# Compressed-branch scores of a two-layer decoder trunk: from eight fp32r matmuls against zero-padded keys to four native fp32 matmuls of 32 columns

## The chip, the cores and the metric

One core of one Trainium2 chip runs the kernel. The time is the device time of one execution in microseconds; lower is better. The kernel before took 349.9 us (median of 3 runs, 349.83 to 349.91).

## What is computed

A decoder trunk of two layers over 256 tokens of width 1024, all in float32. Layer 0 is native sparse attention (16 heads of 64, in 4 groups of 4 heads that share keys and values), layer 1 is a gated linear recurrence (HGRN2). The change lies in the compressed branch of layer 0: blocks of 32 keys, 16 apart, are compressed to 15 keys for each group, rotated, and scored against the queries:

```python
k_cmp = rope(compress(kc, pe_k, wk1, wk2), cmp_end)            # 15 keys per group of heads
sc = einsum('bqgrd,bngd->bqgrn', q, k_cmp) * scale             # r: 4 heads of group g
p_c = masked_softmax(sc, cmp_end[None, :] <= t[:, None])
o_c = einsum('bqgrn,bngd->bqgrd', p_c, v_cmp)
o = g0 * o_c + g1 * o_s + g2 * o_w                             # with selected and window branches
```

With 4 blocks of 64 to select and 16 to be selected, the selected branch takes all blocks, so the scores serve the softmax of the compressed branch only.

## The kernel before

The program is one list of steps (`schedule()`, written out by hand), and every engine walks through this list in the same order and does its own part of each step, with semaphores between them. TensorE's part decides the pace. Big projections are done in "fp32r", a format of 4 bytes that TensorE takes in one pass at reduced precision: each operand is split into a high part (a ScalarE copy, `w_hi`, L889) and a low part (a VectorE subtraction, `w_lo`, L1103), and three matmuls hi·hi, hi·lo, lo·hi are added in PSUM (steps `pa` with 512 moving columns, `pb` with 256). A weight unit is 1024x512, loaded by SyncE into one of two raw buffers and split in four quarters. When a quarter's two parts are ready, `lo_done` counts up, and TensorE's matmuls of that quarter wait for it. `SPREAD` says after which step of the list each quarter is split.

The queries are rotated by VectorE, GpSimd and ScalarE (`rp`, `stg`) and turned by TensorE in the steps `stage`; ScalarE copies them to `q2[128, head, token]`, whose partitions 0 to 63 hold the high parts of the 64 dimensions of a head and 64 to 127 the low parts. So one contraction over 128 partitions against a key that stands there twice gives (q_hi + q_lo)·k.

The compressed keys go through these steps: `cmp2` of the keys (VectorE rotates them, then writes the doubled high part and the doubled low part to `kcs`, L1260 and L1262), `kcT` (two transposes on TensorE, L745; eight ScalarE copies of 32 columns to `kc_pad`, L977), and `sc`, once for each tile i of 128 queries (L618, called at the `sc` branch). `kc_pad[128, part, group, 128]` holds, for each group, its 32 key columns at their own place and zeros elsewhere. The zeros are set by a GpSimd memset at the start (L1431). Eight matmuls (4 groups x 2 parts) of 512 moving columns (4 heads x 128 queries) add up in one bank: each writes all 128 output rows, and contributes to the 32 rows of its group.

```python
for g in range(G):
    for part in range(2):
        m = mm(ps[:], kc_pad[:, part, g], q2[:, g * R:(g + 1) * R, i * P:(i + 1) * P],
               g == 0 and part == 0, g == G - 1 and part == 1)
```

The order of the list around it: `cmp2` of the values, `stage` 6 (its queries are the last that tile 0 needs), three slices of the z projection (weight units U_Z0 and U_Z1, 16 slices of 12 matmuls in all, taken one after the other as `filler`), `sc` 0, two slices, `stage` 7, `scT` 0 (transposes of the scores), two slices, `sc` 1, three slices, `scT` 1, three slices, `pcT` 0 (transposes of the probabilities), the first item `s` 0 of the other branches, two slices, `pcT` 1, the items `s` 1 to 3, the last slice, and then the 24 items of the selected and window branches. Steps `sc`, `scT` and `pcT` 0 share bank 7. After `sc` ScalarE copies the scores out (L983), after `scT` VectorE adds the mask and does the softmax (L1280 to L1295) with the exponentials on ScalarE (L990). In VectorE's own order the split of the last quarter of U_Z1 stands right behind the softmax of tile 0.

Other native fp32 matmuls in the kernel: `cmp1` (output in halves of 64 rows, `w` and `zT`), the products with the values (`pv`, `prob_t` and `v_tok`, halves of 64 rows too, and `vc_bd` over all 128), and layer 1's `qa`, `kb`, `attn`. In the trace each native fp32 matmul shows as two weight loads and two matmuls, here called its two passes; a fp32r matmul shows as one.

Of the kernel before, what the change touches and what calls it, by code (L numbers as in the profile page):

```python
# [21 lines left out]
P = 128  # L22
# [5 lines left out]
H, G, R, HD = 16, 4, 4, 64  # L28
CB, CS, NC, NP_ = 32, 16, 15, 32
# [8 lines left out]
F32 = mybir.dt.float32  # L38
FR = mybir.dt.float32r
BF16 = mybir.dt.bfloat16  # L40
U8 = mybir.dt.uint8
ALU = mybir.AluOpType
ACT = mybir.ActivationFunctionType
# [257 lines left out]
def program(nc, t_in, out):  # L301
    with ExitStack() as ctx:
        def sb(name, shape, dt=F32, scope=ctx):
            return scope.enter_context(nc.sbuf_tensor(name, shape, dt))
# [10 lines left out]
        ident = sb("ident", [P, P])  # L315
        ident_r = sb("ident_r", [P, P], FR)
# [21 lines left out]
        nsa = ExitStack()  # L338
# [4 lines left out]
        q2 = sb("q2", [P, H, S], FR, nsa)  # L343
        k2 = sb("k2", [P, 2, 2, G, S], FR, nsa)
        v_tok = sb("v_tok", [P, TT, 2, G, HD], F32, nsa)
        kc_pad = sb("kc_pad", [P, 2, G, P], FR, nsa)
        vc_bd = sb("vc_bd", [P, 2, P], F32, nsa)
        zT = sb("zT", [P, KT, S], F32, nsa)

# [5 lines left out]
        pre = ExitStack()  # L355
# [3 lines left out]
        hidT = sb("hidT", [P, 2, 2, P], F32, pre)  # L359
        kcr = sb("kcr", [P, 3, HD], F32, pre)  # L360
        tri = kcr[:, 0:2].rearrange("p a d -> p (a d)")
        kcs = sb("kcs", [P, 2, P], FR, pre)
        wg = sb("wg", [P, KT, 48], F32, pre)
        wg_hi = sb("wg_hi", [P, KT, 48], FR, pre)
        wg_lo = sb("wg_lo", [P, KT, 48], FR, pre)
# [77 lines left out]
        kc_v = sem("kc_v")  # L443
        zeros = sem("zeros")
# [40 lines left out]
        def taken(key):  # L485
            return drained[USES[key][0]]
# [25 lines left out]
        def bc(ap, n, at):  # L512

            shape = list(ap.shape)
            return ap.unsqueeze(at).broadcast_to(shape[:at] + [n] + shape[at:])
# [100 lines left out]
        def _(pe):  # L616
            def mm(o, lhsT, rhs, start, stop):
                return nc.tensor.matmul(o, lhsT, rhs, start=start, stop=stop, skip_group_check=True)  # L618
# [16 lines left out]
            for n, (step, banks) in enumerate(SCHEDULE):  # L635
                kind = step[0]
                key = bank_key(step)
# [7 lines left out]
                ps = bank[b]  # L645
# [5 lines left out]
                if kind == "hT":  # L651
# [8 lines left out]
                    for j in range(per_bank):  # L660
                        c = (per_bank * q + j) * P
                        m = nc.tensor.transpose(ps[:, j * P:(j + 1) * P], src[:, c:c + P], ident[:])
                elif kind == "gc":
                    pe.wait_ge(ident_in, 16)
                    pe.wait_ge(g_cols_in, 16)
                    m = nc.tensor.transpose(ps[:, 0:KT], g_rows[0:KT], ident[0:KT, 0:KT])
                elif kind == "rs":
                    pe.wait_ge(ones_set, 1)
                    pe.wait_ge(diag_set, TT)
                    for t in range(TT):  # L670
                        m = mm(ps[:, t * P:(t + 1) * P], ones, diag[:, t], t == 0, t == 1)
                elif kind == "pa" and step[1] == 0:

                    _, u, t, sl = step
# [6 lines left out]
                    for j, kk in enumerate(two):  # L681
# [3 lines left out]
                        m = mm(ps[:], h_lo[:, kk, t * P:(t + 1) * P], w_hi[:, u, kk], False, kk == KT - 1)  # L685
                elif kind == "pa":

                    _, u, t, sl = step
                    if sl == 0:
                        act_ready(0 if u <= U_O1 else 1, t, u)  # L690
                    for kk in (2 * sl, 2 * sl + 1):
# [4 lines left out]
                        m = mm(ps[:], h_lo[:, kk, t * P:(t + 1) * P], w_hi[:, u % 2, kk], False, kk == KT - 1)  # L696
                elif kind == "pb":

                    _, u, m2, sl = step
# [4 lines left out]
                    for kk in range(4 * (sl % 2), 4 * (sl % 2) + 4):  # L704
# [5 lines left out]
                        m = mm(o, cols(w_lo), h_hi[:, kk], False, kk == KT - 1)  # L710
                elif kind == "stage":
# [5 lines left out]
                    for c in range(4):  # L717
                        m = nc.tensor.transpose(ps[:, c * P:(c + 1) * P].bitcast(FR), stg[:, j % 2, 4 * half + c], ident_r[:])  # L718
                elif kind == "cmp1":
# [5 lines left out]
                    for j in range(CS):  # L725
                        half = slice((j % 2) * HD, (j % 2 + 1) * HD)
                        m = mm(ps[half, 0:CH], flat[:, kv, j].rearrange("p g n -> p (g n)"), w1[:, j], j < 2, j >= CS - 2)
                elif kind == "cmpT":
# [4 lines left out]
                    for c in range(2):  # L733
                        m = mm(ps[:, c * HD:(c + 1) * HD], hid[:, c * P:(c + 1) * P], fold[:], c == 0, c == 1)
                elif kind == "cmp2":
# [4 lines left out]
                    for c in range(2):  # L740
                        m = mm(ps[:, 0:HD], hidT[:, kv, c], w2[:, kv, c], c == 0, c == 1)
                elif kind == "kcT":
                    pe.wait_ge(kc_v, 1)
                    for c in range(2):
                        m = nc.tensor.transpose(ps[:, c * P:(c + 1) * P].bitcast(FR), kcs[:, c], ident_r[:])  # L745
                elif kind == "gl":
                    pe.wait_ge(wg_lo_d, 1)
                    for kk in range(KT):
                        mm(ps[0:48, 0:S], wg_hi[:, kk], h_hi[:, kk], kk == 0, False)
                        mm(ps[0:48, 0:S], wg_hi[:, kk], h_lo[:, kk], False, False)  # L750
                        m = mm(ps[0:48, 0:S], wg_lo[:, kk], h_hi[:, kk], False, kk == KT - 1)
                elif kind == "glT":
                    wait_taken(pe, ("gl",))
                    for t in range(TT):
                        m = nc.tensor.transpose(ps[:, t * 48:(t + 1) * 48], gT[:, t * P:(t + 1) * P], ident[0:48, 0:48])
                elif kind == "sc":
                    i = step[1]
# [3 lines left out]
                        for half in range(2):  # L761
                            wait_taken(pe, ("stage", j, half))
                    for g in range(G):
                        for part in range(2):
                            m = mm(ps[:], kc_pad[:, part, g], q2[:, g * R:(g + 1) * R, i * P:(i + 1) * P],
                                   g == 0 and part == 0, g == G - 1 and part == 1)
                elif kind == "scT":
                    i = step[1]
                    wait_taken(pe, ("sc", i))
                    for r in range(R):  # L770
                        m = nc.tensor.transpose(ps[:, r * P:(r + 1) * P], s_ct[:, r * P:(r + 1) * P], ident[:])
                elif kind == "pcT":
                    i = step[1]
                    pe.wait_ge(cmp_scaled, i + 1)
                    for r in range(R):
                        m = nc.tensor.transpose(ps[:, r * P:(r + 1) * P], s_c[:, i, r * P:(r + 1) * P], ident[:])
                elif kind == "s":
                    i, gp, g, rp_, br = ITEMS[step[1]]
# [11 lines left out]
                    if i == 0:  # L790
                        m = mm(ps[:], ident_b[:], bc(tri_b[:], 4, 1), False, True)
                    else:
                        m = mm(ps[:].rearrange("p (r k q) -> p r k q", r=2, k=2)[:, :, 1], ident_b[:], bc(tri_b[:], 2, 1), False, True)
# [84 lines left out]
        def _(act):  # L878
# [26 lines left out]
            for n, (step, _) in enumerate(SCHEDULE):  # L905
                kind, key = step[0], bank_key(step)
                if LAST.get(key) == n:
                    ps = bk(key)
# [50 lines left out]

                            load_w1(act, "v")  # L960
                    elif kind == "cmpT":
                        act.wait_ge(zeros, 3)
                        wait_full(act, key)
                        nc.scalar.activation(hidT[:, step[1]].rearrange("p c (g n) -> p (c g) n", g=G)[:, :, 0:CS],
                                             ps[:, 0:2 * HD].rearrange("p (c n) -> p c n", n=CS), ACT.Silu).then_inc(taken(key), 1)
# [4 lines left out]
                        wait_full(act, key)  # L970
                        nc.scalar.activation(gate[:], ps[:, 0:TT * 48].rearrange("p (t c) -> p t c", t=TT), ACT.Copy).then_inc(taken(key), 1)
                    elif kind == "kcT":
                        act.wait_ge(zeros, 3)
                        wait_full(act, key)
                        for part in range(2):
                            for g in range(G):
                                m = nc.scalar.activation(kc_pad[:, part, g, g * NP_:(g + 1) * NP_],  # L977
                                                         ps[:, part * P + g * NP_:part * P + (g + 1) * NP_], ACT.Copy)
                                if part == 1 and g == G - 1:
                                    m.then_inc(taken(key), 1)  # L980
                    elif kind == "sc":
                        wait_full(act, key)
                        nc.scalar.activation(s_ct, ps[:], ACT.Copy).then_inc(taken(key), 1)  # L983
# [100 lines left out]
        def _(dve):  # L1084
            steps = [0]

            def step_(ins):

                ins.then_inc(vec_step, 1)
                steps[0] += 1  # L1090

            def settled():

                dve.wait_ge(vec_step, steps[0])
# [69 lines left out]
            for n, (step, _) in enumerate(SCHEDULE):  # L1164
                kind, key = step[0], bank_key(step)
                if LAST.get(key) == n:
# [81 lines left out]
                    elif kind == "cmp2" and step[1] == 0:  # L1248
# [6 lines left out]
                        wait_taken(dve, key)  # L1255
                        step_(V.tensor_tensor(kcr[:, 2], kcr[:, 0], kcr[:, 1], ALU.add))
                        settled()
                        hi2 = kcs[:, 0].rearrange("p (u d) -> p u d", u=2)
                        lo2 = kcs[:, 1].rearrange("p (u d) -> p u d", u=2)
                        step_(V.tensor_copy(hi2, bc(kcr[:, 2], 2, 1)))  # L1260
                        settled()
                        V.tensor_tensor(lo2, bc(kcr[:, 2], 2, 1), hi2.bitcast(F32), ALU.subtract).then_inc(kc_v, 1)  # L1262
                    elif kind == "cmp2":
                        dve.wait_ge(zeros, 3)
                        wait_full(dve, key)
                        for g in range(G):
                            m = V.tensor_copy(vc_bd[g * NP_:(g + 1) * NP_, g // 2, (g % 2) * HD:(g % 2 + 1) * HD],
# [159 lines left out]
        def _(pool):  # L1427
            GP = nc.gpsimd
            row = lambda ap: ap.unsqueeze(0).broadcast_to([P, D])
            GP.memset(hidT[:], 0.0).then_inc(zeros, 1)  # L1430
            GP.memset(kc_pad[:].bitcast(F32), 0.0).then_inc(zeros, 1)  # L1431
            GP.memset(vc_bd[:], 0.0).then_inc(zeros, 1)


# [125 lines left out]
```

## Time and profile before

| | before |
|---|---|
| median of 3 runs | 349.9 us (349.83 to 349.91) |
| profiled execution: its own time | 349.11 us |
| its span | 346.5 us |
| TensorE busy | 331.5 us (96%) |
| VectorE busy | 235.4 us (68%) |
| ScalarE busy | 178.4 us (51%) |
| GpSimd busy | 93.2 us (27%) |
| mean granted clock of TensorE | 0.996 of full |

The profiled execution has 2.6 us around its span (349.11 less 346.5), and its own time lies 0.8 us below the median. Starts are counted from the start of the span. A matmul's length in the trace holds its pipeline and overlaps the next ones, so what a matmul costs is read from one start to the next. PE is TensorE, PEld its weight loads, DVE VectorE, ACT ScalarE, POOL GpSimd.

### The profile page before, as it was taken

The page shows a single profiled execution, that of the slowest core. Times are in us where ns is not written, and L with a number is a line of the kernel's source. Part 1 is how long each engine was busy: PE and PEld are TensorE (multiplying, and loading weights), DVE is VectorE, ACT ScalarE, POOL GpSimd, SP SyncE. Part 2 cuts the span into 40 slices and gives each one's busy share as a digit, 9 for nine tenths or more (in the row PEclk, how much of TensorE's full clock was granted, in tenths as well). Part 3 has the DMA queues.
Part 4 walks back from the last instruction along what each step waited for, and adds up shares of the span by engine and source line. Part 5 has one row for each costly group of instructions (what it writes and reads, how often), then busy time and mean ns, then how long its engine had stood idle before and what let it go on. Part 6 is the DMA issues. An engine that isn't in the chain of part 4 may idle for free.

```text
span 346.5 us, 5690 instructions
## 1 busy us (share of the span) xinstructions
PE 331.5 (96%) x2157; PEld 280.7 (81%) x2157; DVE 235.4 (68%) x400; ACT 178.4 (51%) x369; POOL 93.2 (27%) x83
## 2 busy tenths in 40 slices
PE   8999999899799978999999999999999999999993
PEld 5789788678799945676678788999999999889882
DVE  2978957608677498977536835547386996899942
ACT  4966069245561787886517616647353100067621
POOL 2003021523200246574400010050080675533000
PEclk9999999999999999999999999999999999999998
DMA  7999999920747500060530673944636033001011
GB/s 281 380 320 194 329 278 214 316 96 0 163 81 143 103 0 2 13 231 1 193 112 0 215 265 120 311 176 145 214 129 243 1 114 130 2 0 60 3 61 61
DMA packets 28474, 49.37 MB, mean 142 GB/s; under 512 B 3160, under 2 KB 7648, under 8 KB 28448
## 3 DMA queue, kind: packets, MB, share of 16 engines
q1 hardware_dynamic: 25696, 44.82, 41.6%
q10 hardware_dynamic: 2240, 2.17, 3.6%
q0 software_dynamic: 512, 2.03, 1.6%
q8 instruction: 17, 0.28, 0.3%
q14 instruction: 9, 0.07, 0.1%
HBM read 47.97 MB, written 1.05 MB: 141 GB/s over the span
## 4 chain that ended last, share of the span: by engine, by line
PE 73%; DVE 9%; ACT 7%; issue 5%; DMA 2%; POOL 2%; SPq 0%; DVEq 0%; ACTq 0%
PE bank L618 68%; DVE w_lo L1103 4%; PE bank L798 3%; DMA raw<-in_nsa 2%; POOL rp L1450 2%; ACT prob L1009 2%; ACT w_hi L889 2%; ACT h_hi L896 1%; PE bank L718 1%; DVE prob_t L1312 1%; DVE nmax L1300 1%; DVE rp L1211 1%; ACT q L951 1%; ACT w_hi L915 1%; PE bank L859 1%
## 5 line engine op out<-in xcount | busy, mean ns | idle before, releaser
L1103 DVE TENSOR_TENSOR w_lo<-raw,w_hi 128x1024 fp32r<-128x1024 f32 (+1 forms) x80 | 92.8, 1201 | 25.3 <-ACT w_hi L889 25.2
L618 PE MATMUL bank<-w_hi,h_hi 128*128 128x512 f32 x192 | 77.2, 408 | 0.6 <-ACT w_hi L915 0.2
L618 PE MATMUL bank<-w_lo,h_hi 128*128 128x512 f32 x192 | 75.2, 392 | 0.0
L618 PE MATMUL bank<-w_hi,h_lo 128*128 128x512 f32 x192 | 75.1, 391 | 0.0
L889 ACT ACTIVATE w_hi<-raw 128x1024 fp32r<-128x1024 f32 (+1 forms) x80 | 72.6, 968 | 2.0 <-issue 1.9
L618 PE MATMUL bank<-h_hi,w_hi 128*128 128x256 f32 x224 | 64.2, 287 | 0.3 <-DVE w_lo L1103 0.2
L618 PE MATMUL bank<-h_hi,w_lo 128*128 128x256 f32 x224 | 63.4, 283 | 0.0
L618 PE MATMUL bank<-h_lo,w_hi 128*128 128x256 f32 x224 | 63.3, 283 | 0.0
L618 PEld LDWEIGHTS bank<-w_hi,h_hi 128*128 128x128 f32 x192 | 36.0, 188 | 11.3 <-issue 3.4
L618 PEld LDWEIGHTS bank<-h_hi,w_hi 128*128 128x128 f32 x224 | 42.9, 192 | 0.9 <-DVE w_lo L1103 0.7
L539 POOL TENSOR_TENSOR prob<-prob,scl 128x512 f32<-128x512 f32 x24 | 30.3, 1263 | 48.5 <-DVE scl L1131 33.2
L618 PEld LDWEIGHTS bank<-h_lo,w_hi 128*128 128x128 f32 x224 | 42.9, 192 | 0.2
L618 PEld LDWEIGHTS bank<-h_hi,w_lo 128*128 128x128 f32 x224 | 42.9, 192 | 0.0
L618 PEld LDWEIGHTS bank<-w_hi,h_lo 128*128 128x128 f32 x192 | 36.0, 188 | 7.7
L618 PEld LDWEIGHTS bank<-w_lo,h_hi 128*128 128x128 f32 x192 | 36.1, 188 | 7.2 <-DVE w_lo L1174 0.9
L1009 ACT ACTIVATE prob<-bank,nmax 128x128 f32<-128x128 f32 (+1 forms) x64 | 26.2, 429 | 11.1 <-DVE nmax L1300 11.0
L618 PEld LDWEIGHTS bank<-qa,kb 128*128 128x128 f32 (+3 forms) x272 | 29.4, 180 | 2.1 <-issue 1.2
L618 PE MATMUL bank<-qa,kb 128*128 128x128 f32 (+3 forms) x272 | 30.0, 265 | 0.0
L1450 POOL TENSOR_TENSOR rp<-rp 128x256 f32<-128x256 f32 (+1 forms) x8 | 10.5, 1313 | 62.6 <-DVE rp L1214 40.2
L1030 ACT ACTIVATE z_hg<-bank 128x512 f32<-128x512 f32 x4 | 2.4, 597 | 36.2 <-PE bank L618 36.2
L1300 DVE TENSOR_REDUCE nmax<-bank 128x2 f32<-128x512 f32 (+1 forms) x24 | 16.4, 683 | 4.9 <-PE bank L618 4.9
L1489 POOL TENSOR_TENSOR kb<-kb,ft 128x512 f32<-128x512 f32 x12 | 15.8, 1318 | 9.1 <-PE bank L618 9.1
(193 smaller groups left out, 456.3 us busy)
## 6 DMA issues: line engine op xcount, KB each, us to landing
raw<-in_hg SPq DMA_DIRECT2D x16, 1024.0 KB, 6.8
raw<-in_nsa SPq DMA_DIRECT2D x12, 1024.0 KB, 10.4
raw<-in_nsa_out SPq DMA_DIRECT2D x8, 512.0 KB, 8.4
raw<-in_hg_out SPq DMA_DIRECT2D x4, 1024.0 KB, 6.3
raw<-in_nsa SPq DMA_DIRECT2D x4, 512.0 KB, 7.0
w<-in_w1k SPq DMA_DIRECT2D x2, 1024.0 KB, 15.2
w<-in_w1v ACTq DMA_DIRECT2D x2, 1024.0 KB, 14.4
x_res<-in_x SPq DMA_DIRECT2D x2, 512.0 KB, 5.7
```

Of the source, the lines that this page charges most:

```text
L539: nc.gpsimd.tensor_tensor(v(pb_), v(pb_), bc(scl[:, it, 0:nb], 512 // nb, 2), ALU.mult).then_inc(scaled, 1)
L618: return nc.tensor.matmul(o, lhsT, rhs, start=start, stop=stop, skip_group_check=True)
L718: m = nc.tensor.transpose(ps[:, c * P:(c + 1) * P].bitcast(FR), stg[:, j % 2, 4 * half + c], ident_r[:])
L798: m = nc.tensor.transpose(ps[:, c * P:(c + 1) * P], prob[:, it % (NS + 1), c * P:(c + 1) * P], ident[:])
L859: m = nc.tensor.transpose(ps[:, j * P:(j + 1) * P], y_hg[:, c, col:col + P], ident[:])
L889: m = nc.scalar.activation(dst, src, ACT.Copy)
L896: nc.scalar.activation(h_hi[:, kk, t * P:(t + 1) * P], ps[:, kk % 2 * P:(kk % 2 + 1) * P], ACT.Copy, scale=g_cols[:, kk:kk + 1]).then_inc( ...
L1009: m = nc.scalar.activation(prob[:, it % (NS + 1), c * w:(c + 1) * w], ps[:, c * w:(c + 1) * w], ACT.Exp, bias=nmax[:, it, c:c + 1], accum_ ...
L1103: m = V.tensor_tensor(lo, src, hi.bitcast(F32), ALU.subtract)
L1300: V.tensor_reduce(nmax[:, it, 0:nb], ps[:].rearrange("p (a b) -> p a b", a=nb), AX.X, ALU.max, negate=True).then_inc(rowmax, 1)
L1450: GP.tensor_tensor(rp[:, 2, 0:w], rp[:, 0, 0:w], rp[:, 1, 0:w], ALU.add).then_inc(r_sum, 1)
L1489: GP.tensor_tensor(half, half, bc(totals(s, hh)[:, :, :, 1], s, 3), ALU.mult).then_inc(kb_up, 1)
```

## The change

The keys are kept in one piece in full float32: `kc_t[128, 128]` replaces `kc_pad`. VectorE writes one doubled copy, TensorE turns it in one transpose, ScalarE copies it in one instruction, and the memset of the padding goes. In `sc` the queries' bits, high and low parts in their 128 partitions, are read as float32, and each group's matmul has a weight of 32 columns and writes the 32 output rows of that group alone.

```diff
-        kc_pad = sb("kc_pad", [P, 2, G, P], FR, nsa)
+        kc_t = sb("kc_t", [P, P], F32, nsa)
...
-        kcs = sb("kcs", [P, 2, P], FR, pre)
+        kcs = sb("kcs", [P, P], F32, pre)
...
                 elif kind == "kcT":
                     pe.wait_ge(kc_v, 1)
-                    for c in range(2):
-                        m = nc.tensor.transpose(ps[:, c * P:(c + 1) * P].bitcast(FR), kcs[:, c], ident_r[:])
+                    m = nc.tensor.transpose(ps[:, 0:P], kcs[:], ident[:])
...
                     for g in range(G):
-                        for part in range(2):
-                            m = mm(ps[:], kc_pad[:, part, g], q2[:, g * R:(g + 1) * R, i * P:(i + 1) * P],
-                                   g == 0 and part == 0, g == G - 1 and part == 1)
+                        rows = slice(g * NP_, (g + 1) * NP_)
+                        m = mm(ps[rows], kc_t[:, rows], q2[:, g * R:(g + 1) * R, i * P:(i + 1) * P].bitcast(F32), True, True)
...
                     elif kind == "kcT":
-                        act.wait_ge(zeros, 3)
                         wait_full(act, key)
-                        for part in range(2):
-                            for g in range(G):
-                                m = nc.scalar.activation(kc_pad[:, part, g, g * NP_:(g + 1) * NP_],
-                                                         ps[:, part * P + g * NP_:part * P + (g + 1) * NP_], ACT.Copy)
-                                if part == 1 and g == G - 1:
-                                    m.then_inc(taken(key), 1)
+                        nc.scalar.activation(kc_t[:], ps[:, 0:P], ACT.Copy).then_inc(taken(key), 1)
...
-                        hi2 = kcs[:, 0].rearrange("p (u d) -> p u d", u=2)
-                        lo2 = kcs[:, 1].rearrange("p (u d) -> p u d", u=2)
-                        step_(V.tensor_copy(hi2, bc(kcr[:, 2], 2, 1)))
-                        settled()
-                        V.tensor_tensor(lo2, bc(kcr[:, 2], 2, 1), hi2.bitcast(F32), ALU.subtract).then_inc(kc_v, 1)
+                        V.tensor_copy(kcs[:].rearrange("p (u d) -> p u d", u=2), bc(kcr[:, 2], 2, 1)).then_inc(kc_v, 1)
...
             GP.memset(hidT[:], 0.0).then_inc(zeros, 1)
-            GP.memset(kc_pad[:].bitcast(F32), 0.0).then_inc(zeros, 1)
             GP.memset(vc_bd[:], 0.0).then_inc(zeros, 1)
```

The waits on `zeros` count to 2 instead of 3. Nothing else moves: the list of steps, banks and weight splits stay as they are.

## Rows read from the trace of the kernel before

**Rows 1.** page, part 1: busy time of each engine, share of the span, instructions
```profile
PE 331.5 (96%) x2157; PEld 280.7 (81%) x2157; DVE 235.4 (68%) x400; ACT 178.4 (51%) x369; POOL 93.2 (27%) x83
```

**Rows 2.** chain of waits, 90 to 136 us: start us, us, what
```profile
90.77 1.08 ACT q L951 x2
...
91.98 4.96 PE bank L618 x32
...
116.28 0.72 PE bank L618 x5
117.02 0.70 DVE nmax L1300
```

**Rows 3.** timeline of TensorE, 90 to 110 us: start, length, instruction, times, idle before
```profile
91.98 2.09 PE L618 MATMUL bank<-q,kc_pad 128*128 128x512 f32 x8 [1.89 <-ACT q L951]
...
93.91 0.28 PE L618 MATMUL bank<-h_hi,w_hi 128*128 128x256 f32 x1
...
100.77 1.99 PE L618 MATMUL bank<-q,kc_pad 128*128 128x512 f32 x8
...
102.60 0.28 PE L618 MATMUL bank<-h_hi,w_hi 128*128 128x256 f32 x1
```

**Rows 4.** instructions of tile kc_pad: least, median, longest ns; first and last start
```profile
L618 PE MATMUL bank<-q,kc_pad x16: 387/392/467, 92.0 to 102.4; 128*128 128x512 f32 x16
L977 ACT ACTIVATE kc_pad<-bank x8: 178/214/252, 71.0 to 71.6; 128x32 fp32r<-128x32 f32 x8
L1431 POOL MEMSET kc_pad<- x1: 955/955/955, 1.2 to 1.2; 128x1024 f32 x1
```

**Rows 5.** timeline of TensorE, 125.9 to 129.5 us
```profile
128.49 0.39 PE L618 MATMUL bank<-tri_b,ident_b 128*128 128x512 bf16 x1
128.81 0.65 PE L618 MATMUL bank<-prob_t,v_tok 128*64 128x256 f32 x4
129.39 0.33 PE L798 MATMUL bank<-ident,prob 128*128 128x128 f32 x1
```

**Rows 6.** timeline of TensorE, 126.90 to 126.95 us
```profile
126.92 0.44 PE L618 MATMUL bank<-prob_t,v_tok 128*64 128x256 f32 x2
```

**Rows 7.** timeline of TensorE, 40.3 to 44.5 us
```profile
40.62 3.67 PE L618 MATMUL bank<-w,zT 128*64 128x256 f32 x32
```

**Rows 8.** timeline of TensorE, 306 to 308 us
```profile
306.66 1.13 PE L618 MATMUL bank<-qa,kb 128*128 128x128 f32 x8
307.62 0.61 PE L618 MATMUL bank<-v_hg,attn 128*128 128x128 f32 x4
```

**Rows 9.** timeline of VectorE, 57 to 63 us
```profile
57.78 0.23 DVE L1260 CAST kcs<-kcr 128x128 fp32r<-128x128 f32 x1
58.05 0.29 DVE L1262 TENSOR_TENSOR kcs<-kcr,kcs 128x128 fp32r<-128x128 f32 x1
58.25 2.35 DVE L1103 TENSOR_TENSOR w_lo<-raw,w_hi 128x1024 fp32r<-128x1024 f32 x2
```

**Rows 10.** chain of waits, 50 to 92 us
```profile
62.13 3.34 POOL rp L1450
...
77.75 0.75 DVE rp L1211
```

**Rows 11.** timeline of TensorE, 66 to 68 us
```profile
67.36 0.36 PE L745 MATMUL bank<-ident_r,kcs 128*128 128x128 f32 x2 [0.96 <-ACT gate L971]
```

**Rows 12.** timeline of ScalarE, 52 to 93 us
```profile
81.11 0.64 ACT L941 ACTIVATE stg<-rp 128x512 fp32r<-128x512 f32 x1 [7.02 <-POOL rp L1450]
```

**Rows 13.** timeline, 90 to 110 us, VectorE
```profile
92.91 2.50 DVE L1103 TENSOR_TENSOR w_lo<-raw,w_hi 128x512 fp32r<-128x512 f32 x4 [3.31 <-ACT w_hi L889]
...
95.54 0.69 DVE L1247 TENSOR_TENSOR zT<-bank,g_row 128x512 f32<-128x512 f32 x1
...
103.85 1.28 DVE L1103 TENSOR_TENSOR w_lo<-raw,w_hi 128x512 fp32r<-128x512 f32 x2
```

**Rows 14.** timeline of TensorE's weight loads, 106.0 to 106.2 us
```profile
106.08 0.19 PEld L618 LDWEIGHTS bank<-h_hi,w_hi 128*128 128x128 f32 x1
```

More of the change, by code:

```diff
@@ L961, in _ @@
                     elif kind == "cmpT":
-                        act.wait_ge(zeros, 3)
+                        act.wait_ge(zeros, 2)
                         wait_full(act, key)
@@ L972, in _ @@
                     elif kind == "kcT":
-                        act.wait_ge(zeros, 3)
                         wait_full(act, key)
-                        for part in range(2):
-                            for g in range(G):
-                                m = nc.scalar.activation(kc_pad[:, part, g, g * NP_:(g + 1) * NP_],
-                                                         ps[:, part * P + g * NP_:part * P + (g + 1) * NP_], ACT.Copy)
-                                if part == 1 and g == G - 1:
-                                    m.then_inc(taken(key), 1)
+                        nc.scalar.activation(kc_t[:], ps[:, 0:P], ACT.Copy).then_inc(taken(key), 1)
                     elif kind == "sc":
@@ L1257, in _ @@
                         settled()
-                        hi2 = kcs[:, 0].rearrange("p (u d) -> p u d", u=2)
-                        lo2 = kcs[:, 1].rearrange("p (u d) -> p u d", u=2)
-                        step_(V.tensor_copy(hi2, bc(kcr[:, 2], 2, 1)))
-                        settled()
-                        V.tensor_tensor(lo2, bc(kcr[:, 2], 2, 1), hi2.bitcast(F32), ALU.subtract).then_inc(kc_v, 1)
+                        V.tensor_copy(kcs[:].rearrange("p (u d) -> p u d", u=2), bc(kcr[:, 2], 2, 1)).then_inc(kc_v, 1)
                     elif kind == "cmp2":
-                        dve.wait_ge(zeros, 3)
+                        dve.wait_ge(zeros, 2)
                         wait_full(dve, key)
```

## The prediction

> **What bounds the kernel now.** I read the page first, then the chain of waits, then the timelines around the steps `kcT` and `sc`, and at last what each late wait of TensorE was released by. The page says that TensorE is busy for 331.5 of 346.5 us [rows 1], so time taken off TensorE is the only kind that can show. Whether it does is a matter of place. In the chain, ScalarE's copy of the last queries ends a wait of TensorE at 91.98; from there the chain lies on TensorE's matmuls until 117.02, where it passes to VectorE and ScalarE for the first items of the other branches [rows 2]. Both `sc` steps, at 91.98 and 100.77 [rows 3], lie in this stretch of 25 us. So a shorter `sc` counts in full until something that TensorE then reaches too early becomes the limit. The granted clock is the upper of its two levels, 2.4 GHz, in all of this stretch, and it stayed there after the idle time of 1.89 us before the first `sc` [rows 3], so I cost nothing by the lower level.
>
> **The price of `sc` now.** The eight matmuls of the second `sc` start at 100.77 and the next step starts at 102.60: 1.83 us. For the first it is 91.98 to 93.91: 1.93 us [rows 3]. That is 16 matmuls in all [rows 4], 0.23 us each.
>
> **The price of `sc` after.** Each `sc` has four native fp32 matmuls, so eight passes of 512 columns. No row has one with 32 weight columns; the nearest are those with 64, whose outputs go to two halves of the rows. First a single pass: full-width passes of 128 columns start 306.66 to 307.62, eight in 0.96 us, 0.12 each [rows 8], so 0.44 to 0.48 for 512 columns. In `cmp1` 32 passes of 256 columns take 3.67 us [rows 7]. If they followed one another as the full-width ones do, they would take 32 x 0.22 = 7.0 us. They take half, so the two halves run side by side: sixteen slots, 0.22 us from one to the next (3.67 less the last one's own 0.4, over 15), each for two passes of 256 columns. For 512 columns a slot is 0.44 us. The short case is the product with the values: four passes (two matmuls, one for each half) start at 128.81 and the next step starts at 129.39 [rows 5]. That is 0.58 us: two slots of 0.22 and 0.14 around them. And it takes longer to get in: the 512-column bf16 matmul ahead of it started at 128.49, 0.32 earlier [rows 5], against the 0.23 that 512 columns take in `sc` now, so 0.09 more. Two of the four passes start together within the first 0.05 us [rows 6].
>
> If four groups of 32 run side by side as two halves of 64 do, `sc` is two slots of 0.44 plus 0.14 plus 0.09 to get in: 1.11 us. The second `sc` gains 1.83 - 1.11 = 0.72 us. The first is entered out of a wait, so the 0.09 falls away: 1.93 - 1.02 = 0.91 us. Sum 1.63 us. The other end is that nothing overlaps, eight slots, 3.7 us for one `sc`: a loss of 3.65 us over both. I take the first end: rows 5 to 7 are the same kind of instruction with the same split of the output rows, only two instead of four, and they run at the full double rate.
>
> **VectorE and `kcT`.** VectorE makes one copy instead of a copy, a wait and a subtraction: the split of weights behind it starts at 58.25 and would start where the subtraction did or a little before, about 57.98 [rows 9], so 0.27 us earlier. This is on the path: the rotation of the next queries follows on VectorE, then GpSimd at 62.13, ScalarE, and the wait of 0.96 us which TensorE has before `kcT` [rows 10, 11]. The wait shrinks by 0.27. `kcT` itself issues one transpose instead of two, some 0.1 us less of TensorE before the rotation of the last queries at 77.75 [rows 10], from which VectorE, GpSimd and ScalarE lead to 91.98. I count 0.3 us for both together, with bounds of 0 and 0.4.
>
> **ScalarE and GpSimd.** Seven of eight small copies of 0.21 us [rows 4] go, less than 0.6 us of ScalarE's queue since they overlap. ScalarE then waits 7.02 us for GpSimd before 81.11 [rows 12], which hides it: nothing. If that cover were gone it would be worth 0.5 us more. The memset of 0.96 us at 1.2 us [rows 4] has nobody who waits for it before 50 us: nothing. One wait less on `zeros` costs nothing either.
>
> **What is late next.** All of 1.63 us does not come through. Slices 9 to 16 of the z projection use U_Z1. The first weights of its last quarter that TensorE needs (third of four blocks of the second slice of U_Z1) are loaded at 106.08 [rows 14], and VectorE finishes this quarter at 103.85 + 1.28 = 105.13 [rows 13]. So TensorE has 0.95 us to spare there. With everything ahead 0.3 us sooner, and 1.63 us off `sc`, TensorE would be there at 104.15. VectorE's split stands behind the softmax of tile 0 in its queue. How much sooner can that be? VectorE's work at 95.54 waits for TensorE's first z rows, which now come 0.9 us sooner, but VectorE is busy with splits until 92.91 + 2.50 = 95.41 [rows 13]: 0.13 us. Behind it VectorE, ScalarE and VectorE follow each other without a gap that TensorE could close. So the quarter is ready at 105.13 - 0.3 - 0.13 = 104.70 and TensorE waits for it for 0.55 us. What comes through is 0.95 + 0.3 + 0.13 = 1.38 us, however short `sc` becomes.
>
> From there it is TensorE again until 117.02, shifted by 1.38 us. The items then form a chain on VectorE and ScalarE whose first link waits for TensorE's scores (117.02 follows directly on the matmul in [rows 2]), so it shifts too, and beyond it the weights are loaded and split at times set by TensorE.
>
> **Sum.** -0.3 (VectorE and `kcT`) - 1.63 (`sc`) + 0.55 (new wait for the weights) = -1.38 us. For the profiled execution: 349.11 - 1.4 = 347.7 (span 345.1). The median shown is 0.8 above that execution, so 349.9 - 1.4 = 348.5 us.
>
> **Rivals.**
> Pairs only. If TensorE's reading of the moving data serves two fp32 streams and not four, `sc` takes four slots: 1.76 + 0.23 = 1.99 us. First `sc` 1.90 against 1.93, second 1.99 against 1.83: +0.13, less 0.3 gives -0.2, 349.7 us. For it: a fp32r matmul moves 512 columns in 0.23, two fp32 streams move twice 512 in 0.44, the same number of bytes per us, which looks like a limit; no row has more. Against it: the full-width fp32 pass alone takes as long, so it may be the array's own pace. Chance 0.14.
>
> Staggered. Each fp32 matmul has two passes on the same columns. If a matmul of another group may not start before the second pass of the one ahead has, the eight passes need five slots: 2.20 + 0.23 = 2.43 us, +0.41 and +0.60 for the two steps, with -0.3 in all +0.7: 350.6 us, slower. It decides from the fourth slot on. In `cmp1` this rule gives nearly the same sixteen slots, so rows 7 can't exclude it; rows 5 and 6 speak against it, since there it would need three slots and begin with one start, not two. Chance 0.09. The Trainium skill says so, in TensorE: Matmul & The Clock Gate, Part 3 under the mechanism: "MATMULs are pc-monotone in start AND end — strict FIFO, no reordering"; by that rule, the sum would be this one.
>
> No overlap among quarters: eight slots, 3.75 us, +3.6 - 0.3 = +3.3, 353.2 us. Only a rule that holds for 32 columns and not for 64 would do it. Chance 0.07.
>
> Overlap as forecast, but the gain is lost behind it: in the chain of the items VectorE and ScalarE, whose own work comes only 0.43 us (0.3 + 0.13) sooner, set the pace instead of TensorE's `s` 1. Then 349.9 - 0.4 = 349.5 us. Against: the wait at 117.02 was ended by TensorE. Chance 0.10.
>
> The forecast has 0.60. Within it, if VectorE's split comes sooner than I think and the new wait vanishes, it is -1.9: 348.0; if the part of VectorE and `kcT` is nothing, -1.1: 348.8.
>
> **How the numbers follow.** About 0.2% (0.7 us) is what a measurement of this kernel can tell from no change. Faster takes the forecast and little of the last rival: 0.64. Same takes the pairs, most of the lost gain: 0.19. Slower takes the staggered and the serial case: 0.17. The range runs from 347.8 (the forecast with the new wait gone and 0.2 to spare) to 350.2, over the pairs and the lost gain; the staggered and the serial case stay out. The forecast's own range is 347.8 to 349.1.
>
> **What the profile would show.** Right: eight passes of each `sc`, four starting together and four 0.44 to 0.5 later, the next step 1.0 to 1.15 us after the first start; a new wait of TensorE for `w_lo` of about 0.5 us near 104.7; before `kcT` a wait of 0.7 instead of 0.96; the chain passing to VectorE near 115.6. Wrong: starts spread over four, five or eight slots, or, with two slots, a gap of TensorE between 105 and 136 that was not there.

## The result and the profile after

The changed kernel took 347.36 us (median of 7 runs, 346.22 to 348.46). The kernel before, run beside it, took 349.28 us (median of 7, 348.02 to 349.91). The ratio is 0.995, with a 95% interval of 0.9926 to 0.9974: 1.75 us faster, between 0.9 and 2.6. The forecast was 348.5 with a range from 347.8 to 350.2, so the direction was right, the gain larger than forecast by 0.35 (by the ratio) to 0.5 us (by the medians), and the time, 1.14 us below the forecast, outside the range.

The page of the changed kernel (span, busy time, granted clock in 40 slices) answers to [rows 1]:

```profile
span 344.6 us, 5678 instructions
...
PE 329.9 (96%) x2156; PEld 278.0 (81%) x2156; DVE 235.1 (68%) x399; ACT 177.8 (52%) x362; POOL 92.3 (27%) x82
...
PEclk9999999999999999999999999999999999999999
```

The span is 344.6 us against 346.5. TensorE is busy for 1.6 us less, and it has one instruction less, not eight: sixteen fp32r matmuls became eight native ones of two passes each, and one transpose went.

TensorE's timeline around the two score steps (start, length, instruction, times) answers to [rows 3]:

```profile
91.15 1.06 PE L618 MATMUL bank<-q,kc_t 128*32 128x512 f32 x8 [1.89 <-ACT q L949]
92.14 0.38 PE L618 MATMUL bank<-h_hi,w_hi 128*128 128x256 f32 x1
...
99.19 1.07 PE L618 MATMUL bank<-q,kc_t 128*32 128x512 f32 x8
100.18 0.38 PE L618 MATMUL bank<-h_hi,w_hi 128*128 128x256 f32 x1
```

The first step lasts from 91.15 to 92.14, 0.99 us (forecast 1.02), the second from 99.19 to 100.18, 1.00 us (1.02 without its way in, which took the 0.09 us of the forecast: the matmul ahead started at 98.98, 0.21 us before the step where 0.12 is usual). Of the eight passes, four start within the first 0.15 us, as this narrow window of the same timeline shows, and the other four 0.43 to 0.47 us after the first:

```profile
91.15 0.64 PE L618 MATMUL bank<-q,kc_t 128*32 128x512 f32 x4 [1.89 <-ACT q L949]
```

A part of the gain is given back right behind the step. The first two matmuls there, in the kernel before and in the changed one:

```profile
93.91 0.28 PE L618 MATMUL bank<-h_hi,w_hi 128*128 128x256 f32 x1
94.02 0.28 PE L618 MATMUL bank<-h_lo,w_hi 128*128 128x256 f32 x1
```

```profile
92.14 0.38 PE L618 MATMUL bank<-h_hi,w_hi 128*128 128x256 f32 x1
92.37 0.28 PE L618 MATMUL bank<-h_lo,w_hi 128*128 128x256 f32 x1
```

The second of them comes 0.22 us after the first, where it came 0.11 us after it before. So each score step costs 0.11 us more than its own length shows, and the prediction has no term for this. It need not be the change of shape: behind the wait at 104.25 (below) the second matmul comes after 0.22 us too.

VectorE's timeline, and TensorE's at the transposed keys, answer to [rows 9] and [rows 11]; the ScalarE copy answers to one of [rows 4]:

```profile
57.26 0.23 DVE L1250 COPY kcs<-kcr 128x128 f32<-128x128 f32 x1
57.40 2.35 DVE L1095 TENSOR_TENSOR w_lo<-raw,w_hi 128x1024 fp32r<-128x1024 f32 x2
```

```profile
66.50 0.33 PE L744 MATMUL bank<-ident,kcs 128*128 128x128 f32 x1 [0.64 <-ACT gate L969]
```

```profile
L972 ACT ACTIVATE kc_t<-bank x1: 260/260/260, 70.2 to 70.2; 128x128 f32<-128x128 f32 x1
```

VectorE's one copy is at 57.26 and the split of weights follows at 57.40. The wait of TensorE before the transpose is 0.64 us instead of 0.96.

The new wait stands where it was forecast. The timeline of all engines at that place (VectorE's half of the last quarter of U_Z1, TensorE's last matmul that doesn't need it, the weight load that does):

```profile
103.52 0.68 DVE L1095 TENSOR_TENSOR w_lo<-raw,w_hi 128x512 fp32r<-128x512 f32 x1
...
103.76 0.28 PE L618 MATMUL bank<-h_hi,w_lo 128*128 128x256 f32 x1
...
104.25 0.19 PEld L618 LDWEIGHTS bank<-h_hi,w_hi 128*128 128x128 f32 x1 [0.42 <-DVE w_lo L1095]
```

The last matmul before it starts at 103.76 and the next at 104.25, 0.49 us where 0.12 is usual; with the 0.11 us behind it, the wait costs 0.48 us. In the chain of waits this stretch has passed from TensorE to VectorE and ScalarE, where [rows 2] had TensorE all the way to 117.02:

```profile
92.08 2.50 DVE w_lo L1095 x4
...
97.03 1.29 DVE w_lo L1095 x2
98.33 0.61 DVE s_c L1268
...
100.41 0.64 ACT s_c L982
...
102.31 0.69 DVE s_c L1283
103.00 1.22 DVE w_lo L1095 x2
104.25 0.98 PE bank L618 x6
105.24 0.44 PE bank L769 x4
```

These are the splits, the softmax of tile 0 (L1268 to L1283, the exponentials on ScalarE) and then the split of the last quarter, as in the working of the prediction. From 104.25 on TensorE leads again.

If the start of each TensorE instruction in this trace is set beside the start of the same one in the trace before, the difference tells where the time went:

| stretch | forecast | measured |
|---|---|---|
| start, over by 8 us | 0 | -0.54 |
| VectorE and `kcT`, to 91.98 | -0.30 | -0.30 |
| first score step, to the second matmul behind it | -0.91 | -0.82 |
| second score step, with its way in, to the second matmul behind it | -0.72 | -0.64 |
| new wait for U_Z1's last quarter | +0.55 | +0.48 |
| all other stretches together | 0 | -0.06 |
| sum | -1.38 | -1.88 |

Without the start it is -1.34 us against a forecast of -1.38. The sum is closer than its terms because the wait caps it: the score steps gave 0.17 us less than forecast, and in return the wait took 0.07 us less and the other stretches gave 0.06. So two things were left to explain: the 0.54 us at the start, where one part of the change (the memset) lies too, and why the medians differ by 1.9 us.

### The profile page after: what moved, and what is told of

It reads as the page before. It is cut to its first block, busy times and chain, and to the rows that moved or that the text cites. A ratio compares the mean times of both kernels' runs of the same rounds, so it can differ in the third digit from the quotient of the medians.

```text
span 344.6 us, 5678 instructions
## 1 busy us (share of the span) xinstructions
PE 329.9 (96%) x2156; PEld 278.0 (81%) x2156; DVE 235.1 (68%) x399; ACT 177.8 (52%) x362; POOL 92.3 (27%) x82
## 4 chain that ended last, share of the span: by engine, by line
PE 69%; DVE 12%; ACT 8%; issue 5%; POOL 2%; DMA 2%; SPq 1%; DVEq 0%; ACTq 0%
PE bank L618 65%; DVE w_lo L1095 5%; PE bank L796 3%; ACT w_hi L887 2%; POOL rp L1437 2%; DMA raw<-in_nsa 2%; ACT prob L1001 2%; ACT h_hi L894 1%; DVE prob_t L1300 1%; DVE nmax L1288 1%; DVE rp L1203 1%; ACT q L949 1%; ACT w_hi L913 1%; PE bank L718 1%; PE bank L857 1%
```

## The experiments

### The same kernel again, and the memset put back

> The changed kernel once more. Theory (the change is worth the steps from 57 us on, 1.35 us, and the 0.54 us at the start of the first profile pair is the landing of the first loads, which differs from execution to execution): 1.35 us, ratio 0.996, and the shift of the first projection matmul against the kernel before is anything between -1 and +1 us. Rival (the removed memset of 0.96 us on GpSimd makes the start itself 0.5 us shorter): 1.9 us, ratio 0.9945, and the shift at the start is again near -0.5 us.

Measured: ratio 0.9945 (0.9924 to 0.9965), 347.48 us (11 runs) against 349.61 (33 runs). So the medians differ by 1.9 us or more once again: the ratio is the rival's, not the 0.996 of the theory. Its trace is 0.46 us ahead of the trace before by 23 us, so the start looked like the rival's too.

```diff
         vc_bd = sb("vc_bd", [P, 2, P], F32, nsa)
+        pad = sb("pad", [P, 2 * G * P], F32, nsa)
...
             GP.memset(hidT[:], 0.0).then_inc(zeros, 1)
+            GP.memset(pad[:], 0.0)
```

> The changed kernel with the memset of 128x1024 float32 on GpSimd put back at its old place (into a tile that nobody reads). Theory: same time as the changed kernel, ratio 0.996 against the kernel before. Rival (the memset costs the start): 0.5 us of the gain is gone, and the first projection matmul starts 0.5 us later than without it.

Measured: ratio 0.9958 (0.9939 to 0.9976), 347.32 us. In its trace TensorE is 0.64 us ahead of the trace before by 44 us, with the memset in place. In a kernel without it (the one with the early split, below) it is 0.02 us behind. The other traces lie 0.20 to 0.58 us ahead there. So the memset is worth nothing that shows, as forecast, and the profiled execution of the kernel before was a late starter: its span, 346.5 us, stands 0.5 above the 346.0 that the same kernel mostly shows when its clock stays up.

That removes the 0.54 us from the change. It leaves 1.34 us in the trace and 1.9 between the medians. The granted clock accounts for most of the difference. Here it is in 40 slices, of the changed kernel run again and of the kernel before with the early split (described below):

```profile
PEclk9999999999899989999999999999999999999998
```

```profile
PEclk9999999999899989999999999999999999999998
```

The clock falls from 2.4 to 1.2 GHz twice within the work, for 3.4 us each. (It also falls in the last microseconds of every trace of the study, from 341 us at the earliest and 348 us at the latest; the last digit of these lines shows it. The first and the second fall are the two ahead of it.) The busy time in four windows, in the changed kernel run again (window, its length, busy time with counts for PE, PEld, DVE, ACT, POOL, then the granted clock, DMA share, GB/s):

```profile
89.00:91.00 2.00, 0.26 (x3) 0.06 (x1) 0.00 (x0) 1.60 (x4) 1.20 (x2) 1.00 1.04 244
91.00:93.00 2.00, 1.85 (x8) 0.23 (x8) 0.93 (x2) 2.00 (x5) 0.37 (x1) 0.55 1.04 219
93.00:95.00 2.00, 2.00 (x14) 1.99 (x11) 1.57 (x3) 1.92 (x3) 0.00 (x0) 0.60 1.08 225
95.00:97.00 2.00, 2.00 (x21) 2.00 (x19) 0.89 (x2) 1.09 (x4) 0.00 (x0) 1.00 1.07 213
```

TensorE had been idle for 1.9 us, waiting for the last queries; the clock falls at 91.2 us, just as the score step begins, and rises at 94.6. The score step lasts twice as long:

```profile
91.15 1.93 PE L618 MATMUL bank<-q,kc_t 128*32 128x512 f32 x8 [1.89 <-ACT q L949]
93.01 0.58 PE L618 MATMUL bank<-h_hi,w_hi 128*128 128x256 f32 x1
```

It is 1.86 us instead of 0.99. The second fall, at 125 us, lies among the items, where VectorE and ScalarE lead: by 135.7 TensorE has made up its loss. Other traces have only the second fall (the ones with the memset and with the early split, whose spans of 344.5 and 344.7 us are in the lower group below), or none.

The spans of the timed executions fall into two groups (counts, ranges and medians):

| kernel | lower group | upper group |
|---|---|---|
| before (50 executions) | 23, 345.8 to 346.5, median 346.0 | 27, 347.4 to 349.2, median 347.6 |
| changed (18) | 11, 344.4 to 344.9, median 344.6 | 7, 345.6 to 345.8, median 345.7 |

That the first fall makes the upper group is read from the two traces taken in upper executions (345.7 and 347.7 us) and from the mean granted clock that each execution comes with: in the kernel before it is 0.985 to 0.991 in all 27 upper executions and 0.992 or more in all 23 lower ones. Of the changed kernel the two ranges overlap (0.987 to 0.995 and 0.992 to 0.999), since a lower execution can have the second fall. Three upper executions of the kernel before, at 349.0 to 349.2 us and a clock of 0.985, stand 1.5 us higher still; no trace shows why.

In the lower groups the change is worth 1.4 us, the forecast number. The first fall costs the kernel before 1.6 us and the changed one 1.1, by the medians of the groups and by the traces alike (1.57 and 1.08). Why the difference: in the trace of the changed kernel run again there is no wait for U_Z1's last quarter, since TensorE, made late by the fall, comes after VectorE is done. The new wait and the fall are not added; one hides 0.5 us of the other. And the kernel before has its median in the upper group, the changed one in the lower.

### The wait taken out before the first score step

```diff
                     for j in range(4 + i, 8, 2):
+                        if j == 6:
+                            for _ in range(8):
+                                mm(ps[:], ident_r[:], q2[:, 0:R, 0:P], True, True)
                         for half in range(2):
                             wait_taken(pe, ("stage", j, half))
```

The bank is then overwritten by the scores.

> The changed kernel with eight fp32r matmuls of 512 columns (identity against queries that lie ready, into the bank that the scores overwrite, 8 x 0.23 = 1.84 us) between the wait for stage 4 and the wait for stage 6, where TensorE otherwise sits idle for 1.9 us before the first score step. Theory (in some executions the clock falls to 1.2 GHz right behind this idle time, and that is what makes two groups of spans, 344.6 and 345.7 us): the upper group is gone, all spans near 344.6 us, some 0.4 us faster on average than the changed kernel. Rival (the fall comes from something else): 4 in 11 executions near 345.7 us as before.

Measured: 346.48 us, ratio 0.9912 (0.9878 to 0.9945). Six executions, with spans of 344.5, 344.6, 344.6, 344.7, 344.9 and 345.3. None is in the upper group (345.6 and more), though 345.3 lies between the two. The average is 344.77 against 345.06, 0.3 us better (0.4 expected).

> The same eight matmuls in the same place in the kernel before. Theory (its spans stand in two groups, 346.0 and 347.6 us, since the same fall costs it 1.6 us where the changed kernel gives 0.5 us of it back in its wait for weights): all spans near 346.0 us, and the changed kernel with the same matmuls is 1.35 us faster, not 1.9. Rival: half of the executions near 347.6 us as before.

Measured: 348.16 us, ratio 0.9964 (0.9942 to 0.9985). Ten of twelve spans lie between 345.9 and 346.6, two at 347.3 and 347.4. Most of the upper group is gone but not all of it, so "all spans" was too much. Its profiled execution has only the second fall:

```profile
PEclk9999999999999989999999999999999999999998
```

With the same matmuls in both, the difference is 348.16 - 346.48 = 1.7 us in the times and 346.25 - 344.65 = 1.6 us in the median spans: between the 1.35 forecast there and 1.9. Filling the idle time thus takes most of the first falls away: in the kernel before 2 of 12 executions are upper, against 27 of 50. Of the changed kernel 0 of 6 against 7 of 18 would be too few to tell alone. What made the two that are left, and why the clock falls in some executions and not in others after the same idle time, is not shown by any run.

### The early split

The new wait was tested by its cause. VectorE has a gap in the softmax of tile 0 while ScalarE does the exponentials; the split of the last quarter goes there.

```diff
                         V.tensor_tensor(sc, sc, bc(cst[:, i, 0], NP_, 2), ALU.add).then_inc(cmp_v, 1)
+                        if i == 0:
+                            split_lo(U_Z1, [3])
...
                 for u, q in SPLIT_LO_AT.get(n, []):
-                    split_lo(u, [q])
+                    if (u, q) != (U_Z1, 3):
+                        split_lo(u, [q])
```

> The changed kernel with VectorE's split of the last quarter of U_Z1 taken out of its place behind the softmax of tile 0 and put into the gap in which VectorE waits for the exponentials of tile 0. Theory (after the change TensorE waits some 0.5 us for this quarter, and nothing else is near): the wait near 104 us goes and the shift there stays at the full 1.77 us of the two score steps, 0.5 us faster than the changed kernel. Rival (behind it something else, the softmax of tile 0 now 0.6 us later, or the items, takes the 0.5 us back): same time as the changed kernel.

Measured: 347.56 us, ratio 0.9945 (0.9922 to 0.9968), which by itself tells nothing from the changed kernel. VectorE's timeline shows the split at its new place, done at 102.1 us:

```profile
100.20 0.69 DVE L1272 TENSOR_TENSOR s_c<-s_c,cst 128x512 f32<-128x512 f32 x1
100.81 1.28 DVE L1095 TENSOR_TENSOR w_lo<-raw,w_hi 128x512 fp32r<-128x512 f32 x2
```

TensorE has no idle time between 92 and 120 us any more. Counted from the start of the projections, this trace gains 1.83 us on the one before (0.03 late there, at 40 us, 1.80 early at the end) against 1.34: 0.5 us, as the theory says. In the lower group its spans are 344.2 to 344.7, median 344.4 (7 executions), in the upper 345.7 to 346.0 (4): 0.2 us better below, nothing above, where the fall takes the place of the wait. The trace shows the theory right; the times show less than half of it.

> The same move of the split in the kernel before, where TensorE comes to this quarter 0.95 us after it is ready. Theory: within 0.1 us of the kernel before. Rival (the move is worth something by itself): 0.3 us or more faster, or slower by the later softmax.

Measured: 349.63 us, ratio 1.0009 (0.9986 to 1.0033). The move alone is worth nothing that shows (the interval goes from 0.5 us faster to 1.2 us slower); that TensorE comes late enough there was read from the trace ahead of the run.

> The changed kernel with both the eight matmuls and the early split of the last quarter of U_Z1. Theory (two independent losses, the fall and the wait for weights): all spans near 344.2 us, fastest of all kernels here, 0.8 to 0.9 us under the changed kernel on average, 0.35 to 0.5 us under the one with the matmuls alone. Rival (the gain of the early split is lost behind it): same spans as with the matmuls alone.

Measured: 346.24 us (6 runs, 345.81 to 346.60), ratio 0.99 (0.987 to 0.9931). Spans 344.0 to 344.8, median 344.45, against 344.65 with the matmuls alone: 0.2 us by the medians and 0.3 by the averages, less than the 0.35 to 0.5 forecast, within what six executions can tell. By the traces, counted from 44 us on, it is 0.56 us: this one gains 1.91 us on the trace before, the one with the matmuls alone 1.35. It is the fastest kernel of the study, 0.6 us under the changed kernel on average of the spans (344.45 against 345.06), where 0.8 to 0.9 was expected. TensorE's timeline around the former idle time:

```profile
89.08 1.99 PE L618 MATMUL bank<-q,ident_r 128*128 128x512 f32 x8
91.05 1.07 PE L618 MATMUL bank<-q,kc_t 128*32 128x512 f32 x8
```

### Four groups at once

```diff
-                    for g in range(G):
+                    for g in (0, 1, 2, 3, 0, 1, 2, 3):
                         rows = slice(g * NP_, (g + 1) * NP_)
```

> The changed kernel with all four groups of a score step computed twice (eight native fp32 matmuls, the same result). Theory (four groups run side by side, two slots of 0.43 to 0.45 us for a set of four): a score step is 0.88 us longer, 1.88 us from its first start to the next step's, and the second set's passes start in two more bundles of four. Rival (the start times are only queue entries and the array works off one or two groups at a time): 1.8 us or more longer.

Measured, TensorE's timeline:

```profile
91.26 1.92 PE L618 MATMUL bank<-q,kc_t 128*32 128x512 f32 x16 [1.89 <-ACT q L949]
93.12 0.39 PE L618 MATMUL bank<-h_hi,w_hi 128*128 128x256 f32 x1
```

A step lasts 1.86 us, 0.87 more than 0.99. The sixteen passes start in four bundles of four, 0.43 us apart.

```diff
-                    for g in range(G):
+                    for g in (1, 2, 3, 0, 0, 0, 0, 0):
                         rows = slice(g * NP_, (g + 1) * NP_)
```

> The changed kernel with the four groups once and group 0 four more times into the same 32 rows (eight matmuls too, the same result). Theory (only different column groups overlap): the five matmuls of group 0 stand one behind the other, ten slots: a score step is 8 x 0.44 = 3.5 us longer, 4.5 us in all. Rival (it is the number of matmuls, not their place, that counts): 0.88 us longer, as with all four groups twice.

Measured, TensorE's timeline:

```profile
91.23 4.50 PE L618 MATMUL bank<-q,kc_t 128*32 128x512 f32 x16 [1.89 <-ACT q L949]
95.66 0.38 PE L618 MATMUL bank<-h_hi,w_hi 128*128 128x256 f32 x1
```

The step lasts 4.43 us, 3.44 more, and the passes of the repeated group start 0.43 us apart one by one. The same number of matmuls, the same shapes, 2.6 us between the two: different column groups overlap fully, the same group not at all. The pairs, the staggered and the serial rival fall with these two rows. The Trainium skill's rule (TensorE: Matmul & The Clock Gate, Part 3, strict FIFO), read as the prediction read it for the two passes of one matmul, asks for five slots; this trace has two, and the measurement decides. (The trace doesn't tell in which order the two passes of the four matmuls were queued, so it is this reading of the rule that falls.)

### VectorE's operation put back

```diff
+                        step_(V.tensor_copy(hi_x[:].rearrange("p (u d) -> p u d", u=2), bc(kcr[:, 2], 2, 1)))
+                        settled()
                         V.tensor_copy(kcs[:].rearrange("p (u d) -> p u d", u=2), bc(kcr[:, 2], 2, 1)).then_inc(kc_v, 1)
```

> The changed kernel with VectorE's first operation for the keys put back: a copy to fp32r of 128x128 that nobody reads, and the wait for it, ahead of the one copy that is left. Theory (0.27 us of VectorE are on the path to the wait of TensorE before the transposed keys): the wait of TensorE before that transpose is 0.93 to 0.97 us again instead of 0.64, and the shift from there on is 0.27 us smaller. Rival (the 0.3 us at 67 us come from TensorE's one transpose less, or from ScalarE): the wait stays at 0.64.

Measured, TensorE's timeline at the transposed keys:

```profile
66.79 0.33 PE L745 MATMUL bank<-ident,kcs 128*128 128x128 f32 x1 [0.93 <-ACT gate L970]
```

The wait is 0.93 us again. Counted from 53 us, TensorE gains 0.06 us on the trace before by 83 us, where the changed kernel gains 0.30. So 0.24 to 0.29 us are VectorE's, and some 0.06 are left for the one transpose less, the seven copies and the semaphore together. That VectorE's part travels by the next queries' rotation is the prediction's reading of the chain; no run tests it.

## Why the prediction was partly wrong

**Right: what bounds it, and the terms of the sum.** The score steps lie on TensorE's path. ("Time taken off TensorE is the only kind that can show" was too narrow, as the prediction's own term for VectorE says.) "If four groups of 32 run side by side as two halves of 64 do" held: two slots, 0.43 us each. The measured terms are within 0.1 us of the forecast ones, each score step giving 0.08 to 0.09 us less for what follows behind it, and their sum is within 0.04, helped by the cap. The new wait came at the quarter named and cost 0.48 us of the 0.55 forecast. VectorE's 0.27 us went through to TensorE. The memset was worth nothing that shows; the copies and the semaphore were not tested by themselves.

**Wrong: the clock.** The step that made the gain too small (1.4 us, where the medians differ by 1.9) is "so I cost nothing by the lower level". It was read from one execution in which the clock stayed at 2.4 GHz behind the idle time of 1.89 us. In 27 of 50 executions of this kernel the span stands 1.6 us higher, and the two traces taken in upper executions (one of the changed kernel, one of the kernel before with the split moved) show the clock at 1.2 GHz for 3.4 us soon after that idle time, from 91.2 and from about 93 us. The change does not shorten the idle time, but it lessens what the fall costs (1.1 instead of 1.6 us, since the new wait is hidden by it), and its share of upper executions is smaller (7 of 18), though these counts are too few to call that share shown. By the groups: 1.4 us for all, 0.5 x about 0.5 for the smaller cost, 0.15 x 1.1 for the share: 1.8 us, against 1.9 between the average spans (346.98 and 345.06). The part of the 0.15 may be luck.

**Wrong: the base.** The other step that failed is "so 349.9 - 1.4 = 348.5 us". 349.9 was the median of three runs, and they were high ones: with four more it was 349.28, and 33 later ones had 349.61, from 347.77 to 351.56. This is the larger part of the miss: 0.62 of the 1.14 us, and 0.52 are the gain. The root is the same, the clock. Of the 50 executions with a span on record those of the lower group took 347.75 to 349.07 us and those of the upper 349.24 to 351.85. So by their times all three runs of the base (349.83 to 349.91) were of the upper group, while the profiled one, with 349.11 us, a span of 346.5 and no fall ahead of 343 us, stands with the lower. The sum was read from a lower execution and set on a base of upper ones. The prediction noted the 0.8 us and did not ask why. Three runs that agree within 0.1 us had looked like a narrow time; in fact the kernel's times spread over 4 us (347.75 to 351.85), and a range in absolute time had to hold this too.

**The chances.** The trace had the overlap of two groups at full rate in two places, and I gave 0.30 to three ways in which four would not overlap. One outcome can't tell whether that was too much; the two runs on the score step rule all three out.

What stays open: why the clock falls in only some executions after the same idle time, whether the changed kernel really meets it less often (with the memset and the early split 15 of 41 upper executions, against 34 of 62 of the kernel before with and without the early split), and why the early split gives 0.5 us in the traces and 0.2 to 0.3 in the spans.

## What to carry to other kernels

Native fp32 matmuls with few output rows can be laid side by side by giving each its own 32 rows: four of them took the time of one, 0.87 us for 512 columns (a step of 0.99 with its ends), where the step of eight zero-padded fp32r ones took 1.83 to 1.93. After pricing such a gain, look for the next wait TensorE will meet (here weights split behind a softmax), and expect it to cap the gain at the slack that the trace shows. And before a gain of a microsecond is read from medians, look at the span and clock of every execution: this kernel has two groups 1.6 us apart, and filling 1.9 us of idle time of TensorE took most of the upper one away. Three runs that agree can all be of one group.

## What the runs showed of the hardware that was not expected

- After 1.9 us without a matmul the granted clock fell to 1.2 GHz in some executions and not in others. In the profiled ones where it fell within the work (twice at the first place, five times at the second) it did so for 3.4 us each time, beginning between 91 and 94 us or between 123 and 128 us, behind waits of TensorE of 1.9 us at the first place and of 1.0 and 1.3 us at the second.
- At 1.2 GHz a score step of four column groups takes 1.86 us, against 0.99.
- The same fall cost 1.6 us in one kernel and 1.1 in the other, and nothing in the end at the second place, where VectorE and ScalarE lead: the 1.6 us that TensorE is late there are made up by 136 us.
- Behind a score step of four column groups, and behind a wait, the second 256-column matmul comes 0.22 us after the first, against 0.11 to 0.12 otherwise.
- Four streams of float32 into four column groups run at full rate: 4 x 512 columns in 0.43 us for each pass. That is twice the bytes in the same time that one fp32r stream moves (512 columns in 0.23 us), so the rate of one fp32r stream is no limit of what TensorE can read.
